# A two-layer hybrid kernel: what stands between the projection, the chunked scan and the middle product, put in another place

## The reference, cut to what matters

```
h = _f32(_rmsnorm(x, ab_norm_g[i]))
proj = h @ _f32(ab_w_in[i])                    # 1024 x 1024 by 1024 x 6680
z_a, xbc, dt_raw, z_b, q, k, v, ig, fg, og = jnp.split(proj, AB_SPLITS, axis=-1)
# SSD, one step per chunk: y_diag + y_off + xs * d_skip, gated by silu(z_a), group norm
y_off = jnp.einsum('blgn,bgrpn->blgrp', c_c, state) * jnp.exp(acs_c)[..., None]
new_state = state * jnp.exp(acs_c[:, -1])[..., None, None] + \
    jnp.einsum('blgn,blgr,blgrp->bgrpn', b_c, to_end, xdt_c)
# mLSTM, one step per chunk
s = jnp.einsum('bthd,bshd->btsh', q_c, k_c) * w_intra
num = jnp.einsum('btsh,bshv->bthv', s, v_c) + \
    w_inter[..., None] * jnp.einsum('bthd,bhdv->bthv', q_c, c_mem)
c_new = dec[..., None, None] * c_mem + jnp.einsum('bsh,bshd,bshv->bhdv', g, k_c, v_c)
...
y = jnp.concatenate([y_a, y_b], axis=-1) @ _f32(ab_w_out[i])     # the middle product
x = x + y
```

## Time and profile before

| | us |
|---|---|
| median of 3 runs | 1629.3 (1628.87 to 1629.96) |
| the profiled execution's own time | 1628.29 |
| its span in the profile | 1626.6 |
| TensorE busy | 1546.7 (95% of the span) |
| VectorE, ScalarE, GpSimd busy | 899.4, 649.4, 584.1 |
| the last matmul of the projection to the first of chunk 0's `outputs` | 574.0 to 600.0 |
| the last state update of chunk 7 to the middle product's start | 773.9 to 792.7 |

### The profile page before, as it was taken

One profiled execution on the slowest core, in us unless ns is written; L12 is line 12 of the kernel. 1 busy time (PEld: TensorE's weight loads), 2 busy tenths in 40 slices (PEclk: granted clock), 3 DMA queues, 4 the chain that ended last, 5 costly groups with the idle time before them and its releaser, 6 DMA issues.

```text
span 1626.6 us, 23740 instructions
## 1 busy us (share of the span) xinstructions
PE 1546.7 (95%) x9153; PEld 1328.2 (82%) x9153; DVE 899.4 (55%) x1466; ACT 649.4 (40%) x1272; POOL 584.1 (36%) x333
## 2 busy tenths in 40 slices
PE   6899999999999979999699999999999999999797
PEld 5688989898999967778588877888888888877686
DVE  5766878584944338888445434345545234563633
ACT  5443434352532214434243433335554433555421
POOL 4335444444444326565454531124122113221110
PEclk9999999999999979999799999999999999999899
DMA  4124232333333254566385531013112102103622
GB/s 159 52 73 135 86 122 95 113 115 93 117 104 104 72 188 162 165 197 199 123 282 193 171 104 53 26 34 97 53 33 65 33 14 69 68 28 123 237 74 104
DMA packets 149756, 176.36 MB, mean 108 GB/s; under 512 B 8590, under 2 KB 125458, under 8 KB 148626
## 3 DMA queue, kind: packets, MB, share of 16 engines
q1 hardware_dynamic: 149650, 174.91, 32.7%
...
## 4 chain that ended last, share of the span: by engine, by line
PE 46%; DVE 2%; ACT 1%; DMA 1%; issue 1%; POOL 1%; SPq 0%; POOLq 0%; ACTq 0%; DVEq 0%
PE a_ps L2195 21%; PE a_ps L2240 4%; PE a_ps L2215 3%; PE a_ps L2146 3%; PE a_ps L2147 3%; PE a_ps L2148 3%; PE a_ps L2227 2%; PE a_ps L2307 2%; PE a_ps L2308 2%; PE a_ps L2309 2%; PE a_ps L2248 1%; POOL a_w_lo L1713 0%; PE a_ps L2163 0%; DMA a_q_lo<-z 0%; DMA z<-b_y_T 0%
## 5 line engine op out<-in xcount | busy, mean ns | idle before, releaser
L1713 POOL TENSOR_TENSOR a_w_lo<-b_w_raw,a_w_hi 128x1024 fp32r<-128x1024 f32 x72 | 172.5, 2397 | 376.1 <-DVE a_w_hi L1973 253.6
L352 POOL TENSOR_TENSOR p_w_lo<-b_y_T,p_w_hi 128x1024 fp32r<-128x1024 f32 x60 | 156.2, 2605 | 212.9 <-ACT p_w_hi L411 212.9
L2195 PE MATMUL a_ps<-a_h_hi,a_w_hi 128*128 128x512 f32 x384 | 160.8, 419 | 2.9 <-DVE a_h_lo L1951 2.9
L2195 PE MATMUL a_ps<-a_h_hi,a_w_lo 128*128 128x512 f32 x384 | 151.2, 394 | 0.0
L2195 PE MATMUL a_ps<-a_h_lo,a_w_hi 128*128 128x512 f32 x384 | 150.5, 392 | 0.0
L841 PE MATMUL p_bank<-p_w_hi,p_hi_s 128*128 128x256 f32 x512 | 145.0, 283 | 0.0
L841 PE MATMUL p_bank<-p_w_lo,p_hi_s 128*128 128x256 f32 x512 | 144.9, 283 | 0.0
L841 PE MATMUL p_bank<-p_w_hi,p_lo_s 128*128 128x256 f32 x512 | 144.9, 283 | 0.0
L645 DVE SCALAR_TENSOR_TENSOR b_w_raw<-p_out_raw,p_cols,b_w_raw 128x1024 f32<-128x1024 f32 x60 | 119.8, 2004 | 13.7 <-ACT b_w_raw L442 12.3
L841 PE MATMUL p_bank<-p_w_hi,p_hi 128*128 128x256 f32 x384 | 108.9, 283 | 0.0
L841 PE MATMUL p_bank<-p_w_lo,p_hi 128*128 128x256 f32 x384 | 108.7, 283 | 0.0
...
## 6 DMA issues: line engine op xcount, KB each, us to landing
b_y_T<-in_ab_w_in SPq DMA_DIRECT2D x33, 512.0 KB, 4.4
...
b_w_raw<-in_ab_w_out SPq DMA_DIRECT2D x32, 512.0 KB, 3.8
b_w_raw<-in_c_w_in SPq DMA_DIRECT2D x32, 512.0 KB, 4.1
...
feat<-b_w_raw SPq DMA_DIRECT2D x20, 512.0 KB, 3.4
...
```

What stands on the lines that cost most here:

```text
L352: gp.tensor_tensor(w_lo[s % SLOTS][:, :, :], operand(n, split_of(n, p))[:, :, :], w_hi[s % SLOTS][:, :, :].bitcast(F32), ALU.subtract).the ...
L1713: gp.tensor_tensor(w_lo[:, w, :], w_raw[u % W_RAW][:, :], w_hi[:, w, :].bitcast(F32), ALU.subtract).then_inc(S["l_wlo"], 1)
L2195: mm = pe.matmul(o, x, y, start=(k == 0 and q == 0), stop=(k == KT - 1 and q == 2))
```

## The change

Both joints of the scan, the one with the projection and the one with the middle product, are changed.

- **First joint.** SP loads chunk 0's 16 feature tiles during block 11 of the projection, and in block 12 (the last) its first gate, its key tiles, the constants and, behind the first two of the last stores, its other two gates. They land in buffers that the projection has left by then: `w_raw`, `y_raw`, `y_T`. GpSimd makes the masks in block 2, VectorE makes the head table and chunk 0's tables in block 12 (`first_tables`). TensorE turns chunk 0's x, B and keys ahead of the last product (`first_chunk_turned`) and takes the decays of groups 0 and 1 behind it. PSUM is one tensor `b_ps` over all three parts, so the results stay in their banks. SP no longer waits for the token stores at the projection's end; it waits for them at the scan's start, ahead of chunk 0's values and all of chunk 1.
- **Second joint.** The ring of six split units (`b_w`, and `b_yy` for y) belongs to no part now. In the scan's last chunks all four compute engines split units 0 to 5, and TensorE does the 24 matmuls each of units 0 to 3 (`MID_EARLY`) between and behind the turns of chunk 7, tile 0 of each unit last. SP loads units 2 to 7 there. `layer2` begins with unit 4. Its gains come by a DMA of 1024 single elements (`cols`), where a DMA by rows and a turn on TensorE stood.
- The clean-ups of the two outer contexts of the scan (`c`, `k`) are gone.

Diff, cut to its core:

```diff
+                if n == nb - 2:
+                    for s in (0, 1):
+                        sp.wait_ge(S[f"c_stored{s}"], 16 * 2 * nf)
+                    load_first["features"](sp)
+                if n == nb - 1:
+                    sp.wait_ge(S["l_wlo"], seq(n, "7") + 1)
+                    for r in (0, 2):
+                        sp.wait_ge(S[f"t_stored{r}"], 16 * (nt - 2))
+                    load_first["gate_a"](sp)
+                    sp.wait_ge(S["l_wlo"], seq(n, "5") + 1)
+                    load_first["keys"](sp)
...
+                        if n == nb - 1 and (i, k) == (1, 1):
+                            sp.wait_ge(S["l_wlo"], STEPS)
+                            load_first["gates_b"](sp)
...
+            def first_tables():
+                by_part = ident[:, :].rearrange("p (r s h) -> p s r h", s=2, h=SSD_HEADS)
+                dve.tensor_tensor(keep["heads_of"][:, :, :], by_part[:, 0, :, :], by_part[:, 1, :, :], ALU.add
+                                  ).then_inc(S["heads_ok"], 1)
+                dve.wait_ge(S["heads_ok"], 1)
+                chunk_tables(dve, keep, 0, 0, S)
...
+            def first_chunk_turned(n):
+                pe.wait_ge(chunk["fe_landed"][0], 16)
+                pe.wait_ge(chunk["keys_landed"], 16)
+                for b in (0, 1):
+                    pe.wait_ge(S["d_out"], outs(n, LAST_READ["7"], b))
+                turn_features(pe, ahead["ps"], chunk["first_fe"], ident, S)
+                for b in (0, 1):
+                    pe.wait_ge(S["d_out"], outs(n, LAST_READ["5"], b))
+                turn_groups(pe, ahead["ps"], chunk["first_fe"], ident, S)
+                turn_keys(pe, ahead["ps"], chunk["first_keys"], ident, S)
...
+                    if n == nb - 1 and p == ORDER[-1]:
+                        first_chunk_turned(n)
                     product(n, p)
+
+            for b in (0, 1):
+                pe.wait_ge(S["d_out"], outs(nb - 1, LAST_READ["4"], b))
+            pe.wait_ge(S["masks_ok"], 4)
+            pe.wait_ge(S["sel_ok"], 1)
+            for q in (0, 1):
+                decay_rows(pe, ahead["ps"], keep, 0, q, S)
...
+            for r in ahead["t_stored"]:
+                sp.wait_ge(r, 16 * TOK_BLOCKS)
+            load_values(sp, chunk, tok, 0, 0)
+            load_chunk(sp, chunk, feat, tok, 1, 1)
             over(sp, 0, TILES - 2, body)
-            store_y(TILES - 3, 1)
-            for u in range(W_RAW):
-                load_ahead_w(sp, ahead, w_mid, u)
             for i in (0, 1):
                 sp.wait_ge(S[f"y_out{i}"], 16 * 2)
-            for i in (0, 1):
-                load_ahead_y(sp, ahead, yt, i)
+            for u in range(W_RAW):
+                load_ahead_y(sp, ahead, yt, u)
+                load_ahead_w(sp, ahead, w_mid, u)
+            store_y(TILES - 3, 1)
             store_y(TILES - 2, 0)
-            store_y(TILES - 1, 1)
+            for u in range(W_RAW, UNITS_RING + W_RAW):
+                sp.wait_ge(S["l_wlo"], u - W_RAW + 1)
+                load_ahead_w(sp, ahead, w_mid, u)
+                sp.wait_ge(S["d_ylo"], u - 1)
+                load_ahead_y(sp, ahead, yt, u)
+                if u == UNITS_RING - 1:
+                    store_y(TILES - 1, 1)
...
+                f, kt = feats(n, par), keys(n, par)
+                if behind_first(n):
+                    pe.wait_ge(S["sel_ok"], n + 1)
+                    pe.wait_ge(S["d_cmem"], n * 4)
+                    decays(n, par, 0)
+                    decays(n, par, 1)
+                    pe.wait_ge(fe_landed[par], prior * 16 + 16)
+                    pe.wait_ge(S["d_y"], n * 2)
+                    turn_features(pe, ps, f, ident, S)
+                    pe.wait_ge(S["d_state"], n * 2)
+                    turn_groups(pe, ps, f, ident, S)
+                else:
+                    pe.wait_ge(S["cols_ok"], 1)
+                    pe.wait_ge(S["drow_ok"], 1)
                 decays(n, par, 2)
 
...
+            def mid_products(u, tiles):
+                pe.wait_ge(S["l_wlo"], u + 1)
+                pe.wait_ge(S["d_ylo"], u + 1)
+                for t in tiles:
+                    for j in (0, 1):
+                        c, out = slice(j * BLK, (j + 1) * BLK), ps[:, 2 * t + j, :]
+                        if u == 0 and t == 1:
+                            pe.wait_ge(S["d_state"], 2 * TILES)
+                        pe.matmul(out, y_hi(u)[:, t * P:(t + 1) * P], w_hi[:, slot(u), c], start=(u == 0), stop=False)
+                        pe.matmul(out, y_hi(u)[:, t * P:(t + 1) * P], w_lo[:, slot(u), c], start=False, stop=False)
+                        mm = pe.matmul(out, y_lo(u)[:, t * P:(t + 1) * P], w_hi[:, slot(u), c], start=False, stop=False)
+                return mm
+
             over(pe, 0, TILES - 1, body)
             outputs(TILES - 1, 1, (TILES - 1) // 2)
+
+            pe.wait_ge(S["d_cmem"], 4 * TILES)
+            for u in (0, 1):
+                mid_products(u, (2, 3, 1))
             pe.wait_ge(S["d_y"], 2 * TILES)
             turn(TILES - 1, 0)
+            mid_products(2, (2, 3, 1))
             turn(TILES - 1, 1)
+            mid_products(3, (2, 3, 1))
+            pe.wait_ge(S["d_yT"], 4 * TILES)
+            for u in range(MID_EARLY):
+                mid_products(u, (0,)).then_inc(S["p_w"], 1)
...
+                if isinstance(n, int) and n == TILES - 2:
+                    high_y(0)
...
+            act.wait_ge(S["d_yb"], TILES - 1)
+            high_unit(0)
+            high_y(1)
+            high_unit(1)
             memory_squares(TILES - 1)
+            high_y(2)
+            high_unit(2)
             ssd_squares(TILES - 1)
             ssd_norm(TILES - 1)
+            for u in range(3, UNITS_RING):
+                high_y(u)
+                high_unit(u)
...
+                spare(0)
+                spare(1)
                 gp.wait_ge(S["d_y"], n * 2 + 2)
                 gp.wait_ge(S["l_xd"], n + 1)
                 gp.tensor_tensor(y[:, 0:D], y[:, 0:D], x_tok[:, :], ALU.add).then_inc(S["l_yd"], 1)
...
+                spare(2)
...
+            over(gp, 0, TILES - 1, body)
+            body(TILES - 1, 1, (TILES - 1) // 2, low_unit)
+            for u in range(3, UNITS_RING):
+                low_unit(u)
...
                     dve.tensor_tensor(y[:, c], ps[:, k, :], t1[:, c], ALU.add).then_inc(S["d_y"], 1)
+                    if isinstance(n, int) and n == TILES - 2 and k == 0:
+                        low_y(0)
...
+                if isinstance(n, int) and n == TILES - 1:
+                    low_y(1)
...
+            low_y(2)
             ssd_means(TILES - 1)
             turn(TILES - 1, 0, 1, (TILES - 1) // 2)
+            low_y(3)
             turn(TILES - 1, 1, 1)
+            for u in range(4, UNITS_RING):
+                low_y(u)
 
...
+                sp.dma_start(cols[:, :], norm_g.rearrange("k p -> p k")).then_inc(S["cols_in"], 16)
                 sp.dma_start(g_col[:, :], subln_g.rearrange("a p -> p a")).then_inc(S["const_in"], 16)
             for i, r in enumerate(lams):
...
+            for i in (0, 1):
+                sp.wait_ge(ahead["y_out"][i], 16 * TILES // 2)
+            for u in range(UNITS_RING + W_RAW, MID + W_RAW):
                 if u < MID:
                     load_y(u)
                 load_unit(u)
-                if u == 4:
-                    for i in (0, 1):
-                        sp.wait_ge(ahead["y_out"][i], 16 * TILES // 2)
-                if 4 <= u < 8:
-                    load_row(u - 4)
...
-            low_unit(1)
+            low_unit(UNITS_RING)
             gp.iota(neg_dist[:, :], pattern=[[-1, SEQ]], base=SEQ - P, channel_multiplier=1,
...
 
-            pe.wait_ge(S["rows_in"], 16)
-            pe.wait_ge(S["pool_ok"], 3)
-            pe.transpose(ps[:, 7, 0:KT], row_in[0:KT, :], ident[0:KT, 0:KT]).then_inc(S["rows_T"], 1)
-            pe.wait_ge(S["w_high"], 1)
-            pe.wait_ge(S["a_yhi"], 1)
-            for bank in range(8):
-                if bank == 7:
-                    pe.wait_ge(S["cols_ok"], 1)
-                pe.matmul(ps[:, bank, :], y_hi(0)[:, bank // 2 * P:(bank // 2 + 1) * P],
-                          w_hi[:, slot(0), bank % 2 * BLK:(bank % 2 + 1) * BLK], start=True, stop=False)
-            for u in range(MID - LATE):
+            for u in range(MID_EARLY, MID - LATE):
```

More of the change, by code:

```diff
@@ L164, in projection_ab @@
         rstd = m.sb("rstd", [P, TILES])
-        g_lo = m.sb("g_lo", [P, KT + HK, GATES], F32R)
-        bank = [m.ps(f"bank{i}", [P, 512]) for i in range(8)]
+        g_lo = keep["sel"][:, :].rearrange("p (k g) -> p k g", g=GATES)
+        out_raw = m.sb("out_raw", [P, 4, GAPS + SEQ])
+        bank = [ahead["ps"][:, i, :] for i in range(8)]
         XIN = 4
@@ L2045, in _ @@
             dve.wait_ge(S["iota_ok"], 3)
[L2046 removed]
+            dve.wait_ge(S["cols_in"], 16)
+            for i in range(UNITS_RING + 2, AB_OUT_T + 4):
                 low_y(i)
```

327 lines of the change are left out of this document (179 added, 148 removed).

## The result

The changed kernel takes 1609.96 us, median of 4 runs (1605.48 to 1611.67), against 1629.09 of the kernel before on the same chip (4 runs, 1623.95 to 1629.96): a ratio of 0.9882, interval 0.9860 to 0.9905. The forecast was 1600, range 1594 to 1609. The direction was right and 10 us of the 29 did not come.

The account below looks back on a forecast made before the run. TensorE was taken to bound the stages and nothing the joints, where engines start one after the other. Savings of 12.8 and 16.4 us, 29.2 in all, took the profiled 1628.3 to 1599.1; the median, 1.0 above, was said as 1600, range 1594 to 1609.

Parts of the forecast that it names:

- first joint, to state(0): Projection to scan: chunk 0's `outputs` start at 587.2 instead of 600.00, saving 12.8 us.
- last state update to unit 4: Scan's last state update to unit 4's start: 17.1 us saved before chunk 7's 0.7 comes off.
- 6.92 us at full clock follow: First joint: TensorE's work from the third group of decays to chunk 0's `outputs` takes 6.92 us, giving 587.2.
- Rival A: First joint: the clock still falls there, costing 8 us and giving 1608; chance 0.14.
- The block's start: First joint: the scan starts at 579.1, with 1.5 us taken for the block's end.
- chunk 7's delay: End of scan: chunk 7 gets 0.7 us later through VectorE's low part of y(0), bounds 0 to 3.
- rival B: Supply: unit 3's chain, y(0) or small constants come 3 to 8 us late, 1604 to 1608; chance 0.14.
- The second joint: Scan to middle product: unit 4 starts at 801.6 against 818.00, saving 16.4 us.
- Rival C: Both joints: shorter block ends, no chunk 7 delay, early values; 33.4 us saved, 1595; chance 0.08.
- D: Middle product: moved row loads become its bound, making the kernel slower, 1628 to 1632; chance 0.03.
- E: Second joint: early units wait for y, unit 4 starts as before, only the first joint saved, 1616; chance 0.03.
- The cover in `layer2`: Behind unit 4: loads and constants arrive in time, slack 2.3 us, and the 174 us stretch stays as long.

Follow-up runs that it names:

- e7: Changed kernel with y(0) and y(1) loaded ahead of chunk 7, B and key turns in the scan's gap, chunk 0's fourth decay group early: 1598.3 us, ratio 0.9820.
- e3: Changed kernel plus five useless filler matmuls on TensorE between the turned gains and the third group of decays: 1606.4 us.
- e1: The changed kernel run once more with no edit: 1607.0 us, ratio 0.9871.

## Why the prediction was wrong

By its own sum, 12.8 + 16.4 = 29.2, with chunk 7's 0.7 taken out of the second term (17.1 - 0.7); measured from the marks:

| term | forecast | changed | e7 |
|---|---|---|---|
| first joint, to state(0) | 12.8 | 7.4 | 14.8 |
| chunk 7 | -0.7 | -4.3 | -0.5 |
| last state update to unit 4 | 17.1 | 15.1 | 14.8 |
| rest of the span | 0 | -1.2 | +1.1 |

- **The step that failed first** is "6.92 us at full clock follow". Rival A happened (0.14): the clock fell at 581.0. The first joint came 5.4 us short. About 4.8 of that is the clock, where 8 was the price: at full clock the third group at 580.71, 7.15 us to `outputs` (e3) and the 10.6 us from there to the state update that both the kernel before and e7 take would put state(0) at 598.4, and it was at 603.2. The other 0.6 are the third group's start and the 7.15. The evidence against it had been eight stops of up to 1.1 us in the scan, each alone. The joint had two, 1.05 and 1.01, with 0.4 us of work between, and e3 shows that filling the second keeps the clock up until the next stop. The forecast had both stops in its own text and did not put them side by side. The first stop is the block's end, the second ScalarE's `dec`. The forecast's last sentence said that a fall at one joint would put the time outside of the range, but its own price for A, 1608, lies inside; what went past the edge is A, the late y(0) and the 2 us of the second joint together.
- **The block's start** was right because two errors cancelled. The projection's last product ended 0.8 us later than summed (576.97 for 576.2), and the decays and the block's end took 2.3 and not 1.35 + 1.5.
- **The 6.92 itself** was right by luck. It was read from a steady chunk in which a turn fills TensorE while ScalarE and VectorE make `st`; chunk 0 has no turn there, and stands 2.36 us instead (e3). From the third group to `outputs` at full clock e3 measures 588.24 - 581.09 = 7.15.
- **The mis-sized term** is chunk 7's delay: 0.7, bounds 0 to 3, measured 4.3 (2.6 of load and 1.7 of a fall of the clock that the forecast had not priced there), and in seven of the nine profiles with this load order over 3. The rows for it were there: 4.3 MB at 298 GB/s are 14.4 us from the first issue at 726.6, so by that rate y(0) lands at 741.0 at the soonest (it was there at 743.4), and it is wanted at 741.1. I named this and priced it by VectorE's piece. It was counted a second time as part of rival B (0.14), as if A and B excluded each other; they happened together, and the range had room for one.
- **The second joint** held in its mechanism: first product 1.9 us behind the state update as forecast, clock 1.00. From there to unit 4 it was 27.1 us where 25.1 was forecast, just at the bound of 2 that the forecast had set itself. It is 2.0 short for a stop of 1.0 before the turn (VectorE's 5.96 where 3.17 had been), 0.6 for unit 3, and the pieces around them.
- Rival C did not come; D fell, as there is no wait on the supply behind unit 4 and the small constants held nobody up; E fell with unit 4 at 799.8. The cover in `layer2` held: 159.1 us from unit 4 to the stop behind the middle product, for 159.0.
- **Small slips** of the sums, none of which decides: 799.9 + 1.5 is 801.4 and not 801.6; 1664 elements at 150 per us are 11.1 us and not 11.4; half of 298 GB/s makes 8.6 us per unit in D, so about 1625 and not 1628 to 1632.
- **Right for a wrong reason** would have been e7: it saves 29.0 us to unit 4, the forecast's number, but with a first joint of 14.8 in place of 12.8 and a second of 14.8 in place of 17.1. It has the block's end of 1.05, no stop of 1.0 behind it, and 1.3 before `outputs`, where the change's order at full clock has 1.05, 1.0 and 2.4.

Open stays why y(0) lands at different times (its issue is held for 7.3 to 9.2 us in the profiles, and the delay follows that; from the first load of chunk 7 to its landing the DMAs moved 325 GB/s in e1 and e3, whose delays are small, and 303 to 312 in the others), and what mean time that costs.
